# One layer's attention stage reordered: blocks of the prompt start sooner, and two output chunks' first products move into their loop

## The reference

```
h = rmsnorm(x) * (1 + sc1) + sh1;  proj = h @ w_in        # pool | q | k | v | state
y_a = causal pooling of 4 windows, times w_pool
o = (softmax(q1 k1) - lam * softmax(q2 k2)) v              # 4 heads, T5 bias, causal
y_b = rmsnorm(o) * (1 - lam_init)
y_c = complex state space + GLU
x = x + g1 * (concat(y_a, y_b, y_c) @ w_out)
h2 = rmsnorm(x) * (1 + sc2) + sh2
x = x + g2 * (top-8 of 64 routed experts(h2) + shared expert(h2))
```

## Time and profile before

| | us |
|---|---|
| median of 3 runs | 1848.39 (1844.96 to 1851.11) |
| the profiled execution | 1849.96 |
| its span | 1848.3 |
| TensorE busy | 1725.2 (93%) |
| VectorE busy | 660.2 (36%) |
| ScalarE busy | 354.4 (19%) |
| GpSimd busy | 694.9 (38%) |
| mean granted clock of TensorE | 0.964 of full |

### The profile page before, as it was taken

The page is one execution under the profiler, slowest core; times in us unless marked ns, Lnnn a source line. Parts: engine busy times, 40 slices in busy tenths (PEclk is TensorE's granted clock), DMA queues, the critical chain, the costliest instruction groups (busy, mean ns, idle before and its releaser), DMA issues.

```text
span 1848.3 us, 28422 instructions
## 1 busy us (share of the span) xinstructions
PE 1725.2 (93%) x11373; PEld 1008.0 (55%) x11373; DVE 660.2 (36%) x1638; ACT 354.4 (19%) x799; POOL 694.9 (38%) x754
## 2 busy tenths in 40 slices
PE   6999989899999999999789989988999999999984
PEld 3774775455555555555467557644555555555543
DVE  4876464121213222121488744621212121212126
ACT  3332222111113211111032233111111111111111
POOL 1315005454544544444011420334545454545430
PEclk9998999999999999999789899999999999999996
DMA  9779268998999999999956847699999999999935
GB/s 311 236 256 301 94 273 325 383 366 311 411 397 382 370 376 369 380 358 348 343 172 221 274 140 261 259 417 371 373 369 375 353 380 363 375 357 371 365 148 211
DMA packets 216640, 588.91 MB, mean 319 GB/s; under 512 B 67705, under 2 KB 147277, under 8 KB 162622
## 3 DMA queue, kind: packets, MB, share of 16 engines
q1 hardware_dynamic: 146224, 506.99, 72.2%
q0 software_dynamic: 67232, 79.73, 12.6%
q10 hardware_dynamic: 3054, 0.38, 0.2%
...
## 4 chain that ended last, share of the span: by engine, by line
PE 81%; DMA 7%; DVE 6%; issue 2%; SPq 2%; ACT 1%; POOL 1%; DVEq 0%; ACTq 0%; POOLq 0%
PE ps L1386 37%; PE ps L1399 17%; PE ps L927 8%; PE ps L1093 5%; DMA xg<-hrows,idx_x 4%; PE ps L1286 3%; PE ps L983 2%; DMA ypart<-yrows_k 1%; PE ps L956 1%; SPq L631 1%; PE ps L1339 1%; PE ps L1369 1%; DMA wide<-in_w_ada 1%; PE ps L960 1%; DMA raw<-in_w_ada 1%
## 5 line engine op out<-in xcount | busy, mean ns | idle before, releaser
L1386 PE MATMUL ps<-raw,xTs 128*64 128x256 f32 x6144 | 745.6, 394 | 1.7 <-ACT xTs L1669 1.4
L1386 PEld LDWEIGHTS ps<-raw,xTs 128*64 128x64 f32 x6144 | 418.8, 135 | 269.3 <-issue 38.2
L876 POOL DMA_INDIRECT yrows_k<-ytok,idx_y x192 | 196.3, 1022 | 521.0 <-DVE ytok L2088 477.7
L1399 PE MATMUL ps<-dn,scratch 128*64 128x512 f32 x1536 | 361.7, 592 | 2.0 <-DVE scratch L2092 1.5
L2082 DVE TENSOR_TENSOR scratch<-scratch,ps 128x128 f32<-128x128 f32 x192 | 55.3, 288 | 720.0 <-ACT scratch L1691 719.9
L869 POOL DMA_INDIRECT xg<-hrows,idx_x x192 | 198.7, 1035 | 110.5 <-issue 57.5
L2088 DVE COPY ytok<-ps 128x512 f32<-128x512 f32 x192 | 132.8, 692 | 214.2 <-PE ps L1399 214.2
L1669 ACT ACTIVATE xTs<-ps 128x512 f32<-128x512 f32 x192 | 114.6, 598 | 400.4 <-PE ps L927 400.4
L1399 PEld LDWEIGHTS ps<-dn,scratch 128*64 128x64 f32 x1536 | 107.9, 135 | 146.0 <-issue 111.5
L927 PEld LDWEIGHTS ps<-cst,xg 128*128 128x128 f32 x768 | 81.6, 142 | 176.6 <-issue 145.3
L1691 ACT ACTIVATE scratch<-ps 128x128 f32<-128x128 f32 x192 | 53.4, 278 | 638.4 <-PE ps L1386 638.4
...
...
## 6 DMA issues: line engine op xcount, KB each, us to landing
raw<-in_exp_w_gate SPq DMA_DIRECT2D x128, 1024.0 KB
raw<-in_exp_w_up SPq DMA_DIRECT2D x128, 1024.0 KB
dn<-in_exp_w_down SPq DMA_DIRECT2D x128, 1024.0 KB, 9.2
narrow<-in_w_ada SPq DMA_DIRECT2D x18, 1024.0 KB, 9.4
wide<-in_w_in SPq DMA_DIRECT2D x16, 1024.0 KB, 9.0
wide<-in_w_ada SPq DMA_DIRECT2D x16, 1024.0 KB, 9.3
ypart<-yrows_k SPq DMA_DIRECT2D x16, 1024.0 KB, 12.6
raw<-in_w_ada SPq DMA_DIRECT2D x14, 1024.0 KB, 13.0
```

The lines of the kernel that those rows point to most:

```text
L876: pool.indirect_dma_start(yrows_k.rearrange("t (h d) -> (t h) d", h=2), bass.IndirectOffsetOnAxis(ap=idx_y[:, b:b + 1], axis=0), ytok[n % ...
L1386: ins = mm(ps[64 * h:64 * h + 64, 2 + n % 2, 0:256], xTs[n % 2][:, k % 4, 64 * (k // 4):64 * (k // 4) + 64], w[:, k, h], start=k == 0, sto ...
L1399: ins = mm(ps[64 * h:64 * h + 64, 5 + n % 2, :], actT[:, n % 2, 64 * j:64 * j + 64], dn[n % NDOWN][:, j, 512 * h:512 * h + 512], start=j = ...
```

## The change

- The samples' part: `ada` 7 and 8 come after the third and fourth query instead of the fifth and seventh, `ada` 9 after the sixth, `ada` 10 ahead of the samples' score sums; the columns of q = 7 are turned inside the loop. Two of the `warm` calls become one, `warm(7, 4)` goes. Both first score blocks are computed before the samples' weights, and VectorE scales block 0 while ScalarE takes the samples' exponential. For this `pe64` and `comb` move from `scratch` into rows of `mixT`.
- The prompt loop: `ada` 11 comes ahead of it. VectorE does the weights of block n and then scales block n + 2 (before: scales n + 1, then the weights of n). ScalarE takes the exponentials of n + 2 after the copy of n. The value product of head h stands after `scores` of the next head. The `warm(6, 2)` calls go.
- The first four products of output chunks 1 and 0 (pooled and state rows) move into the loop, ahead of the transposes of blocks 6 and 7. The chunks use banks 5, 7, 0, 1 in place of 0 to 3, the factors banks 2, 3, 4, 6 in place of 4 to 7. Chunks 2 and 3's first halves now both stand ahead of the spread.

```
+OUT_BANK, SPREAD_BANK = [5, 7, 0, 1], [2, 3, 4, 6]
...
-    comb = scratch[0:ROWS, 1800:1800 + NS * HEADS]
-    pe64 = scratch[0:ROWS, 1536:1536 + PAST + 1]
+    pe64 = mixT[0:ROWS, 2:5, :].rearrange("p k t -> p (k t)")[:, 0:PAST + 1]
+    comb = mixT[0:ROWS, 2:5, :].rearrange("p k t -> p (k t)")[:, 2 * T:2 * T + NS * HEADS]
...
             for b in range(NS):
-                if b == 5:
+                if b == 6:
                     W(st_copied)
-                if b in (5, 7):
                     warm(6, 2)
                 if b >= 2:
                     W(dec_products, b - 1)
                         for k in range(2):
                             ins = mm(ps[:, 4 + c, 0:T], gluw[:, k, P * c:P * c + P], zv[:, k, :], start=k == 0, stop=k == 1)
                     ins.then_inc(glu_made.sem, 1)
-                elif b == 4:
+                elif b == 2:
                     W(rows_out, 9)
                     ada(layer, ADA_ATTN, 0)
-                elif b == 6:
+                elif b == 3:
                     ada(layer, ADA_ATTN + 1, 1)
-            W(glu_gate)
-            ada(layer, ADA_ATTN + 2, 5)
+                elif b == 4:
+                    W(glu_gate)
+                    ada_turn(layer, ADA_ATTN, 4, 256)
+                elif b == 5:
+                    ada(layer, ADA_ATTN + 2, 5)
+            ada(layer, ADA_ATTN + 3, 7)
...
             W(dec_products, NS)
             scores(0)
-            ada_turn(layer, ADA_ATTN, 4, 256)
-            ada_turn(layer, ADA_ATTN + 1, 0, 0)
-            ada_turn(layer, ADA_ATTN + 2, 1, 0)
-            warm(7, 4)
+            W(ada_copied, ADA_ATTN + 2)
+            scores(1)
+            W(ada_late, len(ADA_IN) + 1)
+            ada_turn(layer, ADA_ATTN + 1, 4, 256)
+            ada_turn(layer, ADA_ATTN + 2, 5, 0)
             W(comb_ready)
+            W(ada_copied, ADA_ATTN + 4)
             for g in range(PAGES):
                 mm(ps[:, 7, 32 * g:32 * g + 32], pe64[:, P * g:P * g + P], comb[:, :], start=True, stop=True)
             mm(ps[0:NS, 7, 64:96], aps[:, :], comb[:, :], start=True, stop=True).then_inc(dec_weights.sem, 1)
+            W(w32_ready)
             W(ada_late, len(ADA_IN) + 3)
-            scores(1)
-            W(w32_ready)
...
             for b in range(4):
                 decode_values(b)
-            ada(layer, ADA_ATTN + 3, 7)
-
-            for n in range(2 * HEADS):
-                h, i = n // 2, n % 2
-                if n + 2 < 2 * HEADS:
-                    scores(n + 2)
-                if i == 0:
-                    if h >= 1:
-                        W(pv_copied, h)
-                    if ADA_ATTN + 3 + h < WIDE_ADA:
-                        ada_turn(layer, ADA_ATTN + 3 + h, 4, 256)
-                if n >= 1:
-                    W(w_copied, n)
-                    warm(6, 2)
-                W(w_ready, n + 1)
-                for t in range(i + 1):
-                    ins = turn(ps[:, 6, P * t:P * t + P], sbuf_w[:, n % 2, P * t:P * t + P], P)
-                ins.then_inc(w_turned.sem, 1)
-                if i == 0:
-                    if ADA_ATTN + 4 + h < WIDE_ADA:
-                        ada(layer, ADA_ATTN + 4 + h, 7)
-                else:
-                    W(w_copied, n + 1)
-                    W(ada_late, min(len(ADA_IN) + 4 + h, WIDE_ADA - ADA_FIRST))
-                    mm(ps[:, 4, 0:NP_], rowsP[:, 2, P * h:P * h + P], sbuf_wT[:, h % 2, 0, :],
-                       start=True, stop=False)
-                    mm(ps[:, 4, P:NP_], rowsP[:, 3, P * h:P * h + P], sbuf_wT[:, h % 2, 1, P:NP_],
-                       start=False, stop=True).then_inc(pv_made.sem, 1)
-                if n == 1:
-                    for b in range(4, NS):
-                        decode_values(b)
-                elif n == 4:
-                    pe.wait_ge(dec_o_copied.sem, dec_o_copied.by(layer, 1))
-                    for k in range(HEADS):
-                        ins = mm(ps[:, 5, 32 * k:32 * k + 32], od[:, P * k:P * k + P], cst[:, K_SUM:K_SUM + 32], start=True, stop=True)
-                    ins.then_inc(dec_o_turned.sem, 1)
-
-            W(pv_copied, HEADS)
-            W(w_copied, 2 * HEADS)
-            W(o_squared)
-            for h in range(HEADS):
-                ins = mm(ps[32 * h:32 * h + 32, 4, 0:T], ones[:, 0:32], osq[:, h, :], start=True, stop=True,
-                         skip_group_check=True, tile_position=(0, 32 * h))
-            ins.then_inc(o_sums.sem, 1)
-
+            ada(layer, WIDE_ADA - 1, 4)
+            ada_turn(layer, WIDE_ADA - 2, 7, 0)
...
-                    ins = mm(ps[:, c % 4, 0:T], w[:, k, P * (c % 2):P * (c % 2) + P], mixT[:, k, :],
+                    ins = mm(ps[:, OUT_BANK[c % 4], 0:T], w[:, k, P * (c % 2):P * (c % 2) + P], mixT[:, k, :],
                              start=k == out_order[0], stop=k == out_order[-1])
                     if (c, k) == (2, out_order[4]):
                         ins.then_inc(out_first_used.sem, 1)
                 return ins
-            W(pool_mixed, 2)
-            W(ssm_mixed)
+            def prompt_values(h):
+                W(w_copied, 2 * h + 2)
+                if h == 0:
+                    W(ada_copied, WIDE_ADA)
+                else:
+                    W(pv_copied, h)
+                mm(ps[:, 4, 0:NP_], rowsP[:, 2, P * h:P * h + P], sbuf_wT[:, h % 2, 0, :],
+                   start=True, stop=False)
+                mm(ps[:, 4, P:NP_], rowsP[:, 3, P * h:P * h + P], sbuf_wT[:, h % 2, 1, P:NP_],
+                   start=False, stop=True).then_inc(pv_made.sem, 1)
+
+            for n in range(2 * HEADS):
+                h, i = n // 2, n % 2
+                if n + 2 < 2 * HEADS:
+                    scores(n + 2)
+                if i == 0 and h >= 1:
+                    prompt_values(h - 1)
+                if n == 2:
+                    W(ada_late, WIDE_ADA - ADA_FIRST - 1)
+                    ada_turn(layer, WIDE_ADA - 1, 7, 256)
+                elif n == 2 * HEADS - 2:
+                    W(pool_mixed, 2)
+                    W(ssm_mixed)
+                    W(ada_late, WIDE_ADA - ADA_FIRST)
+                    pe.wait_ge(*wide_at(layer, WIDE_OUT))
+                    out_part(1, out_order[:4])
+                elif n == 2 * HEADS - 1:
+                    W(o_ready)
+                    out_part(0, out_order[:4])
+                if n >= 1:
+                    W(w_copied, n)
+                W(w_ready, n + 1)
+                for t in range(i + 1):
+                    ins = turn(ps[:, 6, P * t:P * t + P], sbuf_w[:, n % 2, P * t:P * t + P], P)
+                ins.then_inc(w_turned.sem, 1)
+                if n == 1:
+                    for b in range(4, NS):
+                        decode_values(b)
+                elif n == 5:
+                    pe.wait_ge(dec_o_copied.sem, dec_o_copied.by(layer, 1))
+                    for k in range(HEADS):
+                        ins = mm(ps[:, 5, 32 * k:32 * k + 32], od[:, P * k:P * k + P], cst[:, K_SUM:K_SUM + 32], start=True, stop=True)
+                    ins.then_inc(dec_o_turned.sem, 1)
+
+            prompt_values(HEADS - 1)
+            W(pv_copied, HEADS)
+            W(o_squared)
+            for h in range(HEADS):
+                ins = mm(ps[32 * h:32 * h + 32, 4, 0:T], ones[:, 0:32], osq[:, h, :], start=True, stop=True,
+                         skip_group_check=True, tile_position=(0, 32 * h))
+            ins.then_inc(o_sums.sem, 1)
+
+
             W(biased_ready, 2 * HEADS)
-            for c in range(4):
-                if c % 2 == 0:
-                    pe.wait_ge(*(wide_at(layer, WIDE_OUT) if c == 0 else narrow_at(layer, NARROW_OUT)))
+            pe.wait_ge(*narrow_at(layer, NARROW_OUT))
+            for c in range(2, 4):
                 out_part(c, out_order[:4])
-                if c == 1:
-                    W(o_root)
-                    for h in range(HEADS):
-                        mm(ps[:, 4 + h, 0:T], ones[32 * h:32 * h + 1, :], oroot[32 * h:32 * h + 1, :], start=True, stop=True,
-                           skip_group_check=True, tile_position=(32 * h, 0)).then_inc(o_spread.sem, 1)
+            W(o_root)
+            for h in range(HEADS):
+                mm(ps[:, SPREAD_BANK[h], 0:T], ones[32 * h:32 * h + 1, :], oroot[32 * h:32 * h + 1, :], start=True, stop=True,
+                   skip_group_check=True, tile_position=(32 * h, 0)).then_inc(o_spread.sem, 1)
...
             ada_copy(layer, ADA_ATTN, 0)
             ada_copy(layer, ADA_ATTN + 1, 1)
+            ada_columns(ADA_ATTN, 4, 256)
             ada_copy(layer, ADA_ATTN + 2, 5)
-            ada_columns(ADA_ATTN, 4, 256)
+            ada_copy(layer, ADA_ATTN + 3, 7)
             W(dec_max)
             act_(pe64[:, :], pe64[:, :], ACT.Exp, bias=sm[0:ROWS, 9:10], accum_out=sm[0:ROWS, 10:11])\
                 .then_inc(dec_exp.sem, 1)
-            ada_columns(ADA_ATTN + 1, 0, 0)
-            ada_columns(ADA_ATTN + 2, 1, 0)
+            ada_columns(ADA_ATTN + 1, 4, 256)
```

(52 more changed lines are left out.)

4 lines of the change are left out of this document (2 added, 2 removed).

## The result

The changed kernel takes 1839.16 us (median of 7 runs, 1832.96 to 1841.95), the kernel before 1848.39 (7 runs, 1844.96 to 1855.86): ratio 0.994, interval 0.992 to 0.996. It is faster by 9.2 us. The forecast was 1829. 1839 lies in its whole range (1820 to 1844), 10 us above it, just outside the likeliest case's own 1822 to 1838 and beside rival A's 1840. The profiled execution took 1832.96 us, the shortest of the seven, with a span of 1831.3, so its 17.0 us less than the profiled execution before flatters the change.

What follows compares the result with a forecast made beforehand. TensorE held 81% of the waits; its queue order set the attention stretch's pace. Gain 12.4 us less 2 of deductions, 10.4 per layer, 20.8 for two, took 1849.96 to 1829; range 1820 to 1844.

Steps and rivals of the forecast that it cites:

- likeliest case: Main forecast, attention scores to output projection: 10.4 us gained per layer, 1829 us in total, own range 1822 to 1838, chance 0.76.
- rival A: `ada` loads set the pace: `ada` 10's late load cuts the gain to 5 us per layer, 1840 us; chance 0.12.
- mark 1: Samples' scores summed: start of the sums moves from 160.14 to 159.1, gain 1.0 us, with `ada` 10's load 0.5 late.
- mark 3: Last decode product: 184.63 becomes 176.7, gain so far 7.9 us, values at full clock, 0.7 us waiting for `ada` 11's load.
- mark 4: Sums over head outputs: 202.37 becomes 193.2, gain so far 9.2 us, VectorE the bound, output parts only partly covered.
- Mark 2: Samples' weights in place: 169.4 becomes 165.5, gain so far 3.9 us, the exponential's table load taken as hidden.
- The queue for VectorE: Middle of the prompt loop: VectorE bounds it, 4.65 us per pair of blocks against TensorE's 2.5.
- Mark 5: Chunk 0's last products: end moves from 212.82 to 200.4, gain 12.4 us, VectorE's first scaled head exposed by 0.6.
- deduction for the clock: Half-clock stretch expected near 162 to 169, at the samples' values and `ada` 11: 1 us per layer.
- deduction for late loads: Loads landing somewhat later than computed: 1 us per layer.
- Rival B: Clock falls to half from the samples' weights to the output projection and stays: 4.2 us later per layer, 1858; chance 0.05.
- Rival C: Gain given back in the expert stage as longer waits for gathered rows, 10 us per layer: 1848; chance 0.07.

Runs made afterwards that it cites:

- e2: Changed kernel with eight filler products ahead of `ada` 10; on the medians not told apart from the changed kernel.
- e3: Changed kernel with the last eight value pages and the stores held back until `ada` 10's product is done; stage 3.2 and 2.8 us shorter.
- e8: Kernel of e3 with filler in six thin places; median 1831.7 us, ratio 0.9883 to the kernel before.
- e11: Kernel of e8 with output chunks 1 and 0 back behind the loop, filler at blocks 6 and 7 instead; tail 3.56 us longer, loop 1.2 shorter.
- e1: Changed kernel with `ada` 10 moved behind the samples' weights product; time that of the kernel before, its profiled execution 1861.23 us.
- e6: Changed kernel with each head's value product back behind its own transposes; stage 6.3 and 6.4 us longer, loop 20.94 us.
- e7: Kernel before without the seven filler calls of its prompt loop; stage 2.2 and 2.4 us longer.
- e5: Kernel of e1 with two filler products ahead of each loop transpose but the first; median 6 us below e1, loop 19.03 us.
- e9: Kernel of e8 without the later value pages, so the changed kernel plus filler only; layer 1 stage 65.86 us.
- the repeat: Changed kernel as it stands, run again beside three follow-up kernels; 1837.8 us, ratio 0.9932 to the kernel before.

## Why the prediction came out as it did

Sign, range and rival A's number were right; the likeliest case was 10 us too low. That the measured time lies in the range is owed to rival A, for which the range was widened from 1838 to 1844, and not to the likeliest case's working. Gross forecast per layer: chunk 0's rest 62.35 us after the first query (198.6 less 136.26), measured 70.44 in layer 0. The 8.1 us are 4.8 at mark 1, 1.65 at mark 3, 1.1 at mark 4 and 0.5 at the other two, against 2 that I had deducted; the other 6.1, twice, are the distance from 20.8 to 8.65.

- **Mark 1, the failing step: 22.8 forecast, 27.66 measured, 4.8 late.** "took 10.6 us to land" was the wrong reading. The row is a median over two requests, and the product needs the later one: 14.8 in that same group. After, TensorE had the weights 13.4 us after the first request, and started the product 24.1 us after the first query where I had 20.9, 3.1 late. The other 1.7 is the product at half clock (3.64; in e2's layer 0, with filler in the wait, 1.92). e3 shows what made the half late: the value pages, which I had looked at for the second set of values and not for `ada` 10. That SyncE asks for `w_out` sooner had no part in it.
- **Mark 2, right.** 6.57 us from the sums to the values; 6.4 forecast. The table load came ahead of the exponential, as taken, with 0.19 us of wait behind it.
- **Mark 3, 1.65 late.** From start to start the values took 3.4 us and `ada` 11 2.4, where my sum had 1.8 and 1.85, and 0.7 of waiting for a load that was in time: all of it and more is clock.
- **Mark 4, 1.1 late.** The queue for VectorE held: TensorE waits for its last step on a block's weights (L2021) three times in layer 0, 0.67 to 1.42 us. VectorE's busy share from the third block's scaling to the seventh's weights (178.25 to 193.57) was 83%, not over 90%: 12.69 of 15.32 us, with 1.8 of waiting for the scores of the fifth and sixth block and the rest small gaps between its instructions. The lateness is the clock, at one output part (2.9 instead of 1.8 us from start to start, at 193.73) and the value product ahead of it (1.3 instead of 0.85); together 1.6, and the rest of the loop was 0.5 shorter than forecast. At full clock (e8, with filler) the loop took 15.94, less than the 16.5 forecast. The output parts were "only partly covered", as forecast: e11 shows 1.8 to 2.4 of 3.56 us hidden.
- **Mark 5, right.** 5.73 us, 5.4 forecast, a wait of 0.66 at L1248 where 0.6 was forecast.

Windows of the kernel after for the two places where the clock went to half:

```profile
160.00:174.00 14.00, 11.43 (x68) 5.57 (x72) 5.91 (x34) 4.74 (x14) 14.00 (x29) 0.62 1.07 379
192.40:196.50 4.10, 4.10 (x14) 3.35 (x14) 3.16 (x17) 1.48 (x5) 0.00 (x0) 0.58 0.00 0
```

So the deduction for the clock, 1 us, should have been about 5.4: 1.7 at `ada` 10, 2.1 in the third stretch (1.6 on the values, 0.5 on `ada` 11), 1.6 in the loop (e8's loop, at full clock, is 1.7 shorter). The deduction for late loads, 1 us, should have been 3.1, less 0.7 at `ada` 11, which waited for nothing. The part of my theory by which the wait brings the half clock does not hold alone: with 1.46 us of wait left (e3) and with no wait for the load (e1, 0.51) the clock was at half all the same.

Rival A had the right place and total for a part-wrong reason: its sign, over 2 us of waiting at `ada` 10, was there (5.58 and 4.12), but it charged 6 to the load alone and 1 to the clock, where 3.1 and 5.4 were measured. So its number is in part luck.

Rival B was a real danger, given 0.05: the changed kernel's loop stayed at 0.90, but e1 and e6, one step from it, ran at 0.61 and 0.67 and lost the whole gain. My argument against it, that the clock had stayed at full "though TensorE idled 3.5 us of it", left out that filler stood in those gaps; e7 takes it out and the clock is at 0.56. The Trainium skill, in "TensorE: Matmul & The Clock Gate", section "What's actually happening", says that throttling is the default state and activity releases it: e5, e7 and e8 agree (0.61 to 1.00, 1.00 to 0.56, 0.90 to 1.00). But e1 stood at half through 20 us of which TensorE was busy 19.58, and that sentence does not say why.

Rival C is not seen: the stages' 8.65 us arrive in the medians' 9.2, and the repeat's ratio (0.9911 to 0.9953, 8.7 to 16.5 us) leaves no room for a gain given back.

Left open: what decides whether the clock falls in the rounds of cached keys (lower in layer 0 of e1 and e9 than in layer 1), why it fell at about 181 in e1's loop and only at 192 in that of the kernel after, and what the run to run spread of the expert stage comes from. Filler in those rounds was not tried.
